# Other bank distances between weights and streamed tokens, and another order of 64-byte pieces, in a two-network fp32r kernel

## The reference

```python
for layer in range(2):                       # first network
    x = x + mixer(x)                         # layer 0: HGRN + gMLP; layer 1: MLA + MoBA attention
    x = x + peer_ffn(x)                      # 128*128 experts, 8 heads, 16 of them per head
for l in range(2):                           # second network
    x = x + 0.5 * m[2] * swiglu(modulate(x), ffn1_wi[l], ffn1_wo[l])   # D 1024, D_FF 2816
    ctx = ctx + ...swiglu(...)               # layer 0 only: a second stream of 256 tokens
    x = x + m[5] * mixer_ab(x, ctx)          # layer 0: window attention + gated linear attention; layer 1: pooling
    x = x + 0.5 * m[8] * swiglu(modulate(x), ffn2_wi[l], ffn2_wo[l])
x = rmsnorm(x) * final_g
```

## Time and profile before

| | us |
|---|---|
| median of 2 runs | 3410.88 |
| lowest, highest | 3403.97, 3417.79 |
| the profiled execution's own time | 3413.89 |
| its span, first to last instruction | 3412.2 |
| PE busy | 3119.0 |

### The profile page before, as it was taken

How to read it: one execution, slowest core, us unless ns; L and a number is a source line. 1 busy time by engine, 2 the same in 40 slices (tenths; PEclk the granted TensorE clock), 3 DMA queues, 4 the chain that set the end, 5 groups by cost and what they waited for, 6 DMA issues and landing times. The chain is left out here.

```text
span 3412.2 us, 66107 instructions
## 1 busy us (share of the span) xinstructions
PE 3119.0 (91%) x25254; PEld 3013.7 (88%) x25254; DVE 2148.7 (63%) x3339; ACT 1571.3 (46%) x2653; POOL 609.7 (18%) x478
## 2 busy tenths in 40 slices
PE   8789999999998588999999997999987699899798
PEld 7689999999997488999999997999975689899697
DVE  4659698789864658888856775332255555454654
ACT  4244566644453444466645454222155244443343
POOL 0119700023321017900022222000010100000000
PEclk9889999999998699999999998999997699999899
DMA  5145544488884134544479893222150145455353
GB/s 173 53 155 172 181 145 143 152 276 299 309 303 124 41 124 161 179 160 144 145 241 314 309 311 132 96 98 93 61 164 11 50 136 185 143 186 163 124 191 123
DMA packets 178899, 560.66 MB, mean 164 GB/s; under 512 B 22480, under 2 KB 31440, under 8 KB 178144
## 3 DMA queue, kind: packets, MB, share of 16 engines
q1 hardware_dynamic: 178784, 559.21, 49.2%
HBM read 558.10 MB, written 1.05 MB: 164 GB/s over the span
## 5 line engine op out<-in xcount | busy, mean ns | idle before, releaser
L228 ACT ACTIVATE peer_e_hi<-peer_raw 128x1024 fp32r<-128x1024 f32 x512 | 539.3, 1054 | 355.6 <-PE peer_e_s L1180 178.0
L232 DVE TENSOR_TENSOR peer_e_lo<-peer_raw,peer_e_hi 128x1024 fp32r<-128x1024 f32 x416 | 516.8, 1244 | 275.9 <-ACT peer_e_hi L228 275.5
L232 DVE TENSOR_TENSOR ffn_lo<-ffn_raw,ffn_hi 128x1024 fp32r<-128x1024 f32 x260 | 318.6, 1227 | 499.9 <-ACT ffn_hi L228 499.9
L228 ACT ACTIVATE ffn_hi<-ffn_raw 128x1024 fp32r<-128x1024 f32 x264 | 279.6, 1061 | 546.0 <-PE ffn_acc L2007 343.1
L1226 PE MATMUL peer_e_o<-x_normed,peer_e_hi 128*128 128x256 f32 x2048 | 482.3, 278 | 13.5 <-ACT peer_e_hi L228 9.9
L1228 PE MATMUL peer_e_o<-x_normed,peer_e_hi 128*128 128x256 f32 x2048 | 481.6, 278 | 0.0
L1226 PEld LDWEIGHTS peer_e_o<-x_normed,peer_e_hi 128*128 128x128 f32 x2048 | 387.0, 189 | 14.3 <-ACT peer_e_hi L228 10.3
L232 POOL TENSOR_TENSOR x_normed<-peer_e_h,x_normed 128x256 fp32r<-128x256 f32 x256 | 207.1, 809 | 1038.1 <-ACT x_normed L228 1038.1
L1228 PEld LDWEIGHTS peer_e_o<-x_normed,peer_e_hi 128*128 128x128 f32 x2048 | 387.2, 189 | 0.0
L1998 PE MATMUL ffn_acc<-x_normed,ffn_hi 128*128 128x256 f32 x1408 | 354.9, 283 | 20.8 <-DVE x_normed L318 18.2
L1999 PE MATMUL ffn_acc<-x_normed,ffn_hi 128*128 128x256 f32 x1408 | 351.3, 281 | 0.0
(11 more groups left out here) (580 smaller groups left out, 7391.1 us busy)
## 6 DMA issues: line engine op xcount, KB each, us to landing
peer_raw<-in_l_down SPq DMA_DIRECT2D x256, 512.0 KB, 3.3
peer_raw<-in_l_up SPq DMA_DIRECT2D x256, 512.0 KB, 4.8
ffn_raw<-in_ffn_wi SPq DMA_DIRECT2D x176, 512.0 KB, 3.5
peer_ring<-in_w_mod SPq DMA_DIRECT2D x144, 512.0 KB, 5.2
ffn_raw<-in_ffn_wo SPq DMA_DIRECT2D x88, 512.0 KB, 3.4
l_in_raw<-in_l_w_in SPq DMA_DIRECT2D x39, 512.0 KB, 3.8
peer_q_raw<-in_l_peer_w_query SPq DMA_DIRECT2D x32, 512.0 KB, 4.0
wg_in_raw<-in_w_in SPq DMA_DIRECT2D x26, 512.0 KB, 4.1
```

What stands on the lines that cost most here:

```text
L228: return act.activation(hi, v, ACT.Copy)
L232: return eng.tensor_tensor(lo, v, hi.bitcast(F32), ALU.subtract)
```

## The change

A table gives each stage a number of 64-byte pieces (0 to 7) by which its `hi` and `lo` tiles are moved up, and an order in which a product streams its tokens. What follows the weights stands where it stood (a filler of the rest of the line comes behind `lo`), and the token tiles stay at 192 bytes. So the distance from weights to tokens, 3 pieces before, becomes 3 less the number in the table, modulo 8.

PLAIN is the order of before. PAIRED streams piece 0 of the first 128 tokens, piece 0 of the last 128, piece 1 of the first, and so on (a piece is 16 tokens, 64 bytes); BACK does the same from the last piece to the first. The output in PSUM is written in the same order, so each token's result lands where it did. In `project` the order applies to form "f" alone. Where a stage has two orders, the first is for the scores or first products, the second for the sums or second products. Two small tiles of the routing (`dens`) go into the filler.

```diff
+PIECE = 16
+PLAIN, PAIRED, BACK = "plain", "paired", "back"
+PLACES = {
+    "l0_in": (0, PLAIN), "l0_out": (0, BACK), "peer0_q": (7, PAIRED), "peer0_e": (1, PAIRED, PLAIN),
+    "l1_in": (7, PLAIN), "uq": (0, PLAIN), "l1_out": (5, BACK), "peer1_q": (2, BACK), "peer1_e": (2, PAIRED, PLAIN),
+    "ffn1_0": (3, PAIRED, PLAIN), "wg_in": (0, PLAIN), "wg_out": (7, BACK), "ffn2_0": (4, PAIRED, PLAIN),
+    "ffn1_1": (5, PAIRED, PLAIN), "ffn2_1": (6, PAIRED, PLAIN),
+}
+def in_order(a, order):
+    if order == PLAIN:
+        return a
+    names = " ".join("abc"[:len(a.shape) - 2])
+    paired = a.rearrange(f"p {names} (two l e) -> p {names} l two e", two=2, e=PIECE)
+    if order == PAIRED:
+        return paired
+    return paired[:, ::-1] if len(a.shape) == 2 else paired[:, :, ::-1]
...
+    def weights(self, name, shape):
+        ahead = PLACES[self.name][0] * PIECE
+        if ahead:
+            self.ctx.enter_context(self.nc.sbuf_tensor(f"{self.name}_{name}_ahead", [P, ahead], F32))
+        pair = [self.sb(f"{name}{x}", shape, F32R) for x in ("hi", "lo")]
+        if ahead:
+            self.rest = self.ctx.enter_context(
+                self.nc.sbuf_tensor(f"{self.name}_{name}_rest", [P, LINE // 4 - ahead], F32))
+        return pair
...
+def stream(pe, out, w, x, start, stop, order, lax=True):
+    return pe.matmul(in_order(out, order), w, in_order(x, order), start=start, stop=stop, skip_group_check=lax)
...
-                            mm = multiply(pe, acc[0:m, b % 2, j * T:(j + 1) * T], wh[:, c - c0, js],
-                                          wl[:, c - c0, js], xh, xl, c == 0 and j % 2 == 0, end, lax=True)
+                            mm = multiply(pe, in_order(acc[0:m, b % 2, j * T:(j + 1) * T], order), wh[:, c - c0, js],
+                                          wl[:, c - c0, js], in_order(xh, order), in_order(xl, order),
+                                          c == 0 and j % 2 == 0, end, lax=True)
...
-                    pe.matmul(out, w, K.xp[:, 0, c], start=c == 0, stop=False)
-                    pe.matmul(out, w, K.xp[:, 1, c], start=False, stop=False)
+                    stream(pe, out, w, K.xp[:, 0, c], c == 0, False, score_order, False)
+                    stream(pe, out, w, K.xp[:, 1, c], False, False, score_order, False)
```

More of the change, by code:

```diff
@@ L481, in project @@
         raw, units, last_of, view = stream.ring, stream.units, stream.last_of, stream.view
-        hi = st.sb("hi", [P, pairs, UNIT], F32R)
-        lo = st.sb("lo", [P, pairs, UNIT], F32R)
+        hi, lo = st.weights("", [P, pairs, UNIT])
+        order = PLACES[name][1]
         acc = st.ps("acc", [P, 2, 2 * 512])
@@ L1065, in peer_experts @@
         hi_up, lo_up, hi_h, lo_h, out_sum = (st.sem(x) for x in ("hi_up", "lo_up", "hi_h", "lo_h", "out_sum"))
-        hi = st.sb("hi", [P, 2, D], F32R)
-        lo = st.sb("lo", [P, 2, D], F32R)
+        hi, lo = st.weights("", [P, 2, D])
+        score_order, up_order = PLACES[st.name][1:]
         h = st.sb("h", [P, NK, T])
         choice = st.sb("choice", [P, 3, T])
-        dens = st.sb("dens", [P, 2, TT * PH])
+        dens = st.rest[:, 0:2 * TT * PH].rearrange("p (two a) -> p two a", two=2)
         den, rden = dens[:, 0], dens[:, 1]
@@ L1175, in score @@
                     w = hi[:, k % 2, c * P:(c + 1) * P]
-                    pe.matmul(out, w, K.xp[:, 0, c], start=c == 0, stop=False)
-                    pe.matmul(out, w, K.xp[:, 1, c], start=False, stop=False)
+                    stream(pe, out, w, K.xp[:, 0, c], c == 0, False, score_order, False)
+                    stream(pe, out, w, K.xp[:, 1, c], False, False, score_order, False)
                 pe.wait_ge(lo_sem, n + (1 - before))
                 for c in range(DC):
-                    mm = pe.matmul(out, lo[:, k % 2, c * P:(c + 1) * P], K.xp[:, 0, c], start=False, stop=c == DC - 1)
+                    mm = stream(pe, out, lo[:, k % 2, c * P:(c + 1) * P], K.xp[:, 0, c], False, c == DC - 1, score_order, False)
                 mm.then_inc(product, 1)
@@ L1225, in accumulate @@
                     w = hi[:, k % 2, c * P:(c + 1) * P]
-                    pe.matmul(o_ps[:, c], w, h_hi[:, k % 2], start=first and c % 2 == 0, stop=False,
-                              skip_group_check=True)
-                    pe.matmul(o_ps[:, c], w, h_lo[:, k % 2], start=False, stop=False, skip_group_check=True)
+                    stream(pe, o_ps[:, c], w, h_hi[:, k % 2], first and c % 2 == 0, False, up_order)
+                    stream(pe, o_ps[:, c], w, h_lo[:, k % 2], False, False, up_order)
                 pe.wait_ge(lo_up, n + 1)
                 for c in range(DC):
-                    mm = pe.matmul(o_ps[:, c], lo[:, k % 2, c * P:(c + 1) * P], h_hi[:, k % 2], start=False,
-                                   stop=False, skip_group_check=True)
+                    mm = stream(pe, o_ps[:, c], lo[:, k % 2, c * P:(c + 1) * P], h_hi[:, k % 2], False, False, up_order)
                 mm.then_inc(out_sum, 1)
@@ L1930, in swiglu @@
         raw = st.sb("raw", [P, raws, D])
-        hi, lo = st.sb("hi", [P, 2, D], F32R), st.sb("lo", [P, 2, D], F32R)
+        hi, lo = st.weights("", [P, 2, D])
+        first_order, second_order = PLACES[name][1:]
         g = moving_tile(nc, st.ctx, f"{name}_g", [P, 2, FT, n_s * T])
@@ L1996, in first @@
                         at = out[:, s * T:(s + 1) * T]
-                        pe.matmul(at, w, x.pair[:, 0, c], start=c == 0 and s == 0, stop=False, skip_group_check=True)
-                        pe.matmul(at, w, x.pair[:, 1, c], start=False, stop=False, skip_group_check=True)
+                        stream(pe, at, w, x.pair[:, 0, c], c == 0 and s == 0, False, first_order)
+                        stream(pe, at, w, x.pair[:, 1, c], False, False, first_order)
                 if made:
@@ L2006, in first @@
                     for s, x in enumerate(streams):
-                        mm = pe.matmul(out[:, s * T:(s + 1) * T], w, x.pair[:, 0, c], start=False,
-                                       stop=c == DC - 1, skip_group_check=True)
+                        mm = stream(pe, out[:, s * T:(s + 1) * T], w, x.pair[:, 0, c], False, c == DC - 1, first_order)
                 mm.then_inc(product, 1)
@@ L2026, in second @@
                     for s in range(n_s):
-                        pe.matmul(out_ps(s, c), w, gs(0, s), start=start and c % 2 == 0, stop=False,
-                                  skip_group_check=True)
-                        pe.matmul(out_ps(s, c), w, gs(1, s), start=False, stop=False, skip_group_check=True)
+                        stream(pe, out_ps(s, c), w, gs(0, s), start and c % 2 == 0, False, second_order)
+                        stream(pe, out_ps(s, c), w, gs(1, s), False, False, second_order)
                 pe.wait_ge(lo_2, f + 1)
@@ L2032, in second @@
                     for s in range(n_s):
-                        mm = pe.matmul(out_ps(s, c), lo[:, k, c * P:(c + 1) * P], gs(0, s), start=False,
-                                       stop=False, skip_group_check=True)
+                        mm = stream(pe, out_ps(s, c), lo[:, k, c * P:(c + 1) * P], gs(0, s), False, False, second_order)
                 mm.then_inc(out_sum, 1)
```

## The result

The changed kernel takes 3509.37 us, median of 2 runs (3505.66 to 3513.08), against 3410.88: ratio 1.0289, 95% interval 1.0188 to 1.039. A second comparison, of 4 runs with 7 of the kernel before, gives 1.0238 (1.0203 to 1.0274). The forecast was 3398 with a range up to 3490. The change makes the kernel slower by 2.4 to 2.9%, and the whole interval of the second comparison lies beyond 2%, which the first alone leaves open; the measured time is outside the range.

A forecast was written before the change was run, and what follows sets the result against it. PE, always busy in large stages, was taken as the bound. Paired products gave -13.2 us, other parts nothing: 3413.9 - 13.2 = 3400.7 on the profiled scale, 3.0 above the median, so 3398 us; range 3358 to 3490.

The forecast's parts named there:

- The reading of the floor: Large PE matmuls: weight load sets about 111.7 ns; the 1.7 or 6.1 ns above it is stream and load meeting.
- Paired products hold the quick beat always: Paired stages: every matmul at 113.33 ns, none at the slow 117.8; 13.2 us gained; bounds 111.7 and 117.8 ns.
- Nothing gained or lost: Plain products at new distances keep their share of slow beats: 0 us; all quick -8.1, all slow +31.0.
- rival (4): Plain-order units at new distances: all at the slow 117.8 ns beat, +31 us, 3429 us; chance 0.09.
- BACK at nothing: Small backward products, 16 + 3 x 8 units: no change, with bounds of -1.6 to +4.3 us.
- (1): Paired units: side-by-side reads clear the meeting, steps fall to 111.7 ns, 17 us more gained, 3381 us; chance 0.20.
- (6): All products: no jump penalty and floor steps everywhere, -29.5 - 22.7 us, 3359 us; chance 0.01.
- (2): Whole kernel: nothing moves, each stage's start draws its beat anew, 3411 us within 15; chance 0.13.
- (3): A paired stage at a bad distance: stream meets load in every piece, 53 ns per matmul, 3454 to 3562 us; chance 0.14.
- (5): PSUM output: 16 jumps per matmul at one column each, 6.7 ns, +77 us, 3475 us; two columns 3550; chance 0.05.
- equal excess in all paired stages: Sign in the profile after, across paired stages, that would speak for (5); no size given.
- The forecast fails if some distance has a third, longer step: Failure sign in the profile after: plain stages should step only at 2.72 or 2.83 us per 24 matmuls.

The follow-up runs named there:

- e8: TensorE alone, no network: the sweep of e6 at four distances with loads of 8 and 32 weight columns, further orders, bursts after rest; no total time given.
- e9: TensorE alone, no network, one distance: streams of 64 to 512 columns, pairs or turned-round pieces of several sizes, loads of 128 or 8 columns, fp32 too; 1212.64 us.
- e2: Changed kernel with its orders kept but every distance as in the kernel before: 3479.33 us, ratio 1.0151 to the kernel before.
- e6: TensorE alone, no network: bursts of 72 matmuls of 256 columns, 8 orders at 8 distances, plain and paired also with 64-column loads; 1782.71 us.
- e1: Changed kernel with its distances kept but all orders plain: 3490.05 us, ratio 1.0171 to the kernel before.
- e4: Changed kernel at distance 0 with its orders on the PSUM output alone, tokens streamed plainly: 3426.33 us beside 3425.33 of the kernel before, single run.
- e5: Changed kernel at distance 0 with its orders on the streamed tokens alone, output written plainly: 3473.33 us beside 3427.73 of the kernel before, single run.

## Why the prediction was wrong, by its own steps

- **The reading of the floor** failed first: "I read it as a meeting of the two SBUF reads in the same piece of the line". The excess over 111.7 was compared with rows in which the load is the bound (128 or fewer streamed columns). A stream of 256 columns takes 113.3 with a load of 8 columns too (e8, e9). There was nothing for the paired order to clear.
- **"Paired products hold the quick beat always"**, worth -13.2 us with 117.8 as the bad bound, is the step that fails by most: all seven paired stages step at 120.0, at any distance (e2, e6), and they cost +58.8 us. The bad bound was the worst beat seen in plain order; a paired stream was in no row, and only the load-bound fp32 row stood for it.
- **"Nothing gained or lost" for plain products** also fails: +35.5 us against a bound of +31.0. The size was near to rival (4), but two of the four kinds of distance have steps beyond 117.8, namely 118.7 and 120.0 (e1, e6). "Since the beat differs at one and the same distance" was true and told nothing against distance: both act.
- **BACK at nothing**, with +4.3 as its bound: +4.9.
- **Rivals.** (1) and (6), floors below 113.3, are excluded by e8 and e9. (2) fails: something moved. The rule quoted beside it (the Trainium skill, "TensorE: Matmul & The Clock Gate", "Part 2: What happens when you issue a matmul") fits the price of the order, 120.0 with either load, but not the plain steps, which differ by up to 6.7 ns with the weights' place alone and change with the size of the load (e6). (3), a wait per piece at a bad distance, appears nowhere: it was priced at 53 ns, and the most that any distance adds to 120.0 is 3.2, in the first burst at c and at g (e6). (5) had its signature, "equal excess in all paired stages", and its size, 6.7 ns, with the wrong place: jumps in the output are free (e4), those in the reads pay all (e5). Its rule (the Trainium skill, "PSUM — Partial Sum Buffer", "Specifications (TRN2)") isn't borne out for runs of 64 bytes: e4 took 3426.33 beside 3425.33.
- **Two counts** were off and changed little. Rival (1) takes 88 first-product units for the three one-stream stages, which have 132, so it should have been 19 us and not 17. `l_in` has 144 matmuls of 512 columns and not some 60, and moved by 0.9 us where 0.4 was the bound.
- **What held**: PE is the engine waited for and sets the time; loads, cuts and queues have cover, and PE's idle time didn't grow. "The forecast fails if some distance has a third, longer step": it has, 120.0. The range ended at 3490 because (5) was worked out alone, 3475; together with plain products at bad distances, +35, it would have held 3509. That (5)'s 6.7 ns met the measured excess is luck: it was worked out for jumps in the output.

**What stays open.** Why a stage at the good distance goes at 113.3 or at 117.8, and others at 118.7 or 120.0. Equal code and addresses give different steps (the bursts of e8, and `peer1_q` in the change's two profiles), and within one expert stage the beat changes as well. Some choice at a start or after a wait is a guess; what makes it wasn't found, nor why it turns with each unit beside the routing. How the period of 256 bytes arises inside the chip, and how the place and the size of the load act together, isn't shown either, only that they do.

## What to carry to other kernels

A floor is a floor of the resource that was the bound in that row: before reading an excess as a collision, find a row in which the same operation runs with the other resource idle. Where an access pattern hasn't been timed, bound it by a pattern of its own kind, not by the worst time of the plain one; a few hundred matmuls on an idle core give it in microseconds. And when two parts of a change can each be bad, the upper end of the range must hold both at once.

## What the runs showed of the hardware that wasn't expected

- Plain fp32r streams of 256 columns on an idle core beside loads of 128 columns: steps of 120.0, 113.3, 118.7 or 117.8 ns by the distance from weights to tokens modulo 256 bytes; one place in four is good (e6). With loads of 64 columns another place is good (113.3 where it was 120.0, 119.1 where it was 113.3), and with streams of 512 another again (226.7 to 233.4, e8).
- Streamed reads in pairs of runs: 113.3 ns with runs of 256 bytes, 118.8 with 128, 120.0 with 64, 123.3 with 32 (e9). Those of 64 and 32 bytes took this at every distance but for two first bursts (123.2 with 64), and with the small load too (122.3 at one distance with 32); 128 bytes took 116.7 with the small load and up to 120.0 at another distance, and 256 was timed at the good distance alone. The same 64-byte runs, turned round in one piece, took 117.8 at half of the distances and 120.0 at the others (e6): it matters where the jump goes.
- The output's order in PSUM, in runs of 64 bytes, costs nothing (e4, one run).
- One and the same burst, with the same addresses and nothing beside it, settled at 113.3 once and at 120.0 another time.
